# Recurrent scan in one kernel: key norms kept as twelve columns of tokens, and cumulative differences taken in the middle of the previous block's inversion

## What is computed

```
kk = hs(k0 * k_k)                                   # heads of 64 channels
kk = kk / jnp.maximum(jnp.sqrt(jnp.sum(kk * kk, axis=-1, keepdims=True)), 1e-12)
k  = hs(k0 * (1.0 + (a - 1.0) * k_a))
bonus = jnp.sum(rh * k * r_k, axis=-1, keepdims=True) * vh
# per token, for each direction d:
sa = jnp.einsum('bhij,bhj->bhi', s, kk_t)
s = s * w_t[:, :, None, :] - sa[..., None] * b_t[:, :, None, :] + v_t[..., None] * k_t[:, :, None, :]
y = jnp.einsum('bhij,bhj->bhi', s, r_t)
```

## Time and profile before

| what | value |
|---|---|
| median of 3 runs | 3482.51 us (3479.51 to 3484.06) |
| profiled execution, its own time | 3481.5 us |
| its span | 3479.7 us |
| PE busy | 3148.1 us, 90% |
| DVE busy | 1621.9 us, 47% |
| POOL busy | 1338.8 us, 38% |
| ACT busy | 1193.3 us, 34% |
| scan stage in the span | 2310 to 2930 us |

### The profile page before, as it was taken

How to read it: one execution, slowest core, us unless ns; L and a number is a source line. 1 busy time by engine, 2 the same in 40 slices (tenths; PEclk the granted TensorE clock), 3 DMA queues, 4 the chain that set the end, 5 groups by cost and what they waited for, 6 DMA issues and landing times. The chain is left out here.

```text
span 3479.7 us, 51376 instructions
## 1 busy us (share of the span) xinstructions
PE 3148.1 (90%) x19551; PEld 2515.4 (72%) x19551; DVE 1621.9 (47%) x3054; ACT 1193.3 (34%) x2127; POOL 1338.8 (38%) x880
## 2 busy tenths in 40 slices
PE   6999989799998999899899979995788889979996
PEld 5888865588886888677688858873666666758875
DVE  6444377444435673422621134326666645264443
ACT  3222245422223222234322232243444434343342
POOL 3444431344443434433344432234666630133332
PEclk8999989899998999999899989996999989979998
DMA  7565421365544554222433341222222233111211
GB/s 230 176 190 162 131 70 43 97 187 181 170 144 140 173 159 150 87 86 73 127 92 96 95 140 49 66 87 60 49 52 52 52 102 109 37 54 56 61 49 43
DMA packets 636834, 363.16 MB, mean 104 GB/s; under 512 B 109182, under 2 KB 629108, under 8 KB 636144
## 3 DMA queue, kind: packets, MB, share of 16 engines
q1 hardware_dynamic: 632432, 353.48, 34.3%
q10 hardware_dynamic: 3056, 6.29, 0.5%
q0 software_dynamic: 1168, 0.91, 0.1%
HBM read 334.12 MB, written 26.50 MB: 104 GB/s over the span
## 5 line engine op out<-in xcount | busy, mean ns | idle before, releaser
L266 POOL TENSOR_TENSOR w_lo<-w_raw,w_hi 128x1024 fp32r<-128x1024 f32 (+1 forms) x398 | 939.6, 2362 | 1724.9 <-ACT w_hi L258 1724.9
L303 PE MATMUL acc<-h,w_hi 128*128 128x512 f32 x3136 | 979.2, 393 | 6.7 <-POOL w_lo L266 6.7
L258 ACT ACTIVATE w_hi<-w_raw 128x1024 fp32r<-128x1024 f32 (+1 forms) x398 | 414.5, 1042 | 989.4 <-PE acc L303 961.3
L303 PEld LDWEIGHTS acc<-h,w_hi 128*128 128x128 f32 x3136 | 584.1, 188 | 128.7 <-POOL w_lo L266 7.8
L303 PE MATMUL acc<-h,w_lo 128*128 128x512 f32 x1568 | 613.3, 391 | 0.0
L303 PE MATMUL acc<-hid,w_hi 128*128 128x512 f32 x1408 | 437.1, 392 | 0.0
L303 PE MATMUL lat<-h,w_hi 128*128 128x512 f32 x912 | 336.6, 408 | 19.6 <-DVE h L429 17.5
L303 PEld LDWEIGHTS acc<-h,w_lo 128*128 128x128 f32 x1568 | 294.9, 188 | 63.9
L830 DVE SCALAR_TENSOR_TENSOR ada_part<-ada_raw,c_act,ada_part 128x256 f32<-128x256 f32 x672 | 315.0, 488 | 18.6
L303 PEld LDWEIGHTS acc<-hid,w_hi 128*128 128x128 f32 x1408 | 263.5, 188 | 54.1
L303 PE MATMUL acc<-hid,w_lo 128*128 128x512 f32 x704 | 275.0, 391 | 0.0
(11 more groups left out here) (512 smaller groups left out, 4866.2 us busy)
## 6 DMA issues: line engine op xcount, KB each, us to landing
w_raw<-in_ffn_w SPq DMA_DIRECT2D x240, 512.0 KB, 4.0
ada_raw<-in_ada_w SPq DMA_DIRECT2D x88, 1024.0 KB, 5.0
w_raw<-in_od_w_in SPq DMA_DIRECT2D x32, 512.0 KB, 4.0
w_raw<-in_ev_w_in SPq DMA_DIRECT2D x30, 512.0 KB, 3.9
w_raw<-in_ffn_w SPq DMA_DIRECT2D x32, 384.0 KB, 3.5
image<-inverse_wait SPq DMA_DIRECT2D x288, 32.0 KB, 2.2
first_ada<-in_ada_w SPq DMA_DIRECT2D x8, 1024.0 KB, 12.4
w_raw<-in_ab_w_in SPq DMA_DIRECT2D x16, 512.0 KB, 3.8
```

What stands on the lines that cost most here:

```text
L258: act.activation(K.w_hi[:, first % SPLIT, 0:tiles, :], K.raw[:, first % RAW, 0:tiles, :], ACT.Copy).then_inc(K.hi_ready, 1)
L266: pool.tensor_tensor(K.w_lo[:, first % SPLIT, 0:tiles, :], K.raw[:, first % RAW, 0:tiles, :], K.w_hi[:, first % SPLIT, 0:tiles, :].bitcast ...
L303: mm = pe.matmul(out, w[:, slot, k, :], moving(ap, k, tokens), start=first and k == 0 and p == 0, stop=last and k == tiles - 1 and p == le ...
```

## The change

1. `norm` becomes twelve small products: 64 tokens of `tmp` as the stationary operand, two columns of `bd64` as the moving one, so that tokens lie on partitions and the sums of one block are 12 columns (`inv`, 128x12). ACT's root, DVE's maximum and one reciprocal work on these 12 columns. A new PE operation `spread` (twelve products of a broadcast column with the identity) brings the factors back to PSUM by tiles of 64x128, and DVE multiplies `kk` with them (`unit`) in place of POOL's `kk`. After the root ACT evaluates one sigmoid of a single column (`warm`), for c > 0.
2. POOL's two differences of block `c + 1` are taken in `invert(c)`, after round n = 21 (`2 * N // 3`); for blocks 0 and 1 just ahead of their preparation. POOL's list has nine operations left.
3. The places move: DVE's maximum, reciprocal and sums earlier, `kt` and `k` from n = 16 to 19 to n = 18 to 21, `rk` from 26 to 31, the bonus product on PE from 29 to 32 and the bonus on DVE from 32 to 34; the gates of `decay` on ACT one place earlier, those of `rate` one later (15 and 17). `lora(1, 0)` now waits for DVE's `unit`, and `spread` for `decay1` and `inv`. On ACT the second rate gate of block 0 thereby falls behind `late(1)`.

```diff
-    "pe": ["norm", "decay0", "decay1", "rate0", "rate1", "bonus"],
+    "pe": ["norm", "decay0", "decay1", "spread", "rate0", "rate1", "bonus"],
@@ gpsimd
+                def differences(c):
+                    O = B[c % 3]
+                    for d in range(2):
+                        pool.wait_ge(S.pd, prep("dve", c, f"sum{d}"))
+                        pool.tensor_tensor(O.q[d], O.cs[d], O.q[d], ALU.subtract).then_inc(S.pq, 1)
...
+                        if n == 2 * N // 3 and c + 1 < RB:
+                            differences(c + 1)
                     pool.wait_ge(S.solving, base + 2 * N - 2)
                     pool.sem_inc(S.solved, 1)
...
+                    op("ksum", tmp, O.kt[0], O.kt[1], ALU.add, ("dve", "k1"))
                     for d in range(2):
-                        op(f"before{d}", q[d], O.cs[d], q[d], ALU.subtract, ("dve", f"sum{d}"))
-                    op("kk", kk, kk, tmp, ALU.mult, ("dve", "inv"))
-                    op("ksum", tmp, O.kt[0], O.kt[1], ALU.add, ("dve", "k1"), ("pool", "kk"))
-                    for d in range(2):
-                        op(f"bkk{d}", rate[d], rate[d], kk, ALU.mult, ("dve", f"kt{d}"), ("pool", "kk"))
+                        op(f"bkk{d}", rate[d], rate[d], kk, ALU.mult, ("dve", f"kt{d}"))
...
+                split("before0")
+                differences(0)
                 prepare(0, split)
...
+                differences(1)
                 prepare(1)
@@ tensor
                     if n == 6:
-                        product(K.bd64, lambda sl: tmp[:, sl], act("square"), *([(S.low_copied, c * 2 * PAIRS)] if c else []))
-                    if n == 9:
+                        pe.wait_ge(*act("square"))
+                        if c:
+                            pe.wait_ge(S.low_copied, c * 2 * PAIRS)
+                        for ch in range(NCH):
+                            for m, a in enumerate(SIDES):
+                                half = slice(ch * CH + 64 * m, ch * CH + 64 * m + 64)
+                                mm = pe.matmul(prep_bank[a, 0, 2 * ch:2 * ch + 2], tmp[:, half], K.bd64[:, 0:P:64],
+                                               start=True, stop=True)
+                        mm.then_inc(S.pp, 1)
+                    if n == 8:
                         lora(0, 0, (S.lw, c * 64 + 64), act("root"))
-                    if n == 11:
+                    if n == 10:
                         lora(0, 1, act("decay0"))
-                    if n == 13:
-                        lora(1, 0, act("decay1"))
-                    if n == 15:
+                    if n == 12:
+                        pe.wait_ge(*act("decay1"))
+                        pe.wait_ge(S.pd, prep("dve", c, "inv"))
+                        for ch in range(NCH):
+                            for h, a in enumerate(SIDES):
+                                mm = pe.matmul(prep_bank[a, ch // 3, ch % 3 * CH:ch % 3 * CH + CH],
+                                               inv[:, 2 * ch + h:2 * ch + h + 1].broadcast_to([P, 64]), K.ident,
+                                               start=True, stop=True)
+                        mm.then_inc(S.pp, 1)
+                    if n == 14:
+                        lora(1, 0, (S.pd, prep("dve", c, "unit")))
+                    if n == 16:
                         lora(1, 1, act("rate0"))
-                    if n == 29:
+                    if n == 32:
                         product(K.bd64, lambda sl: tmp[:, sl], act("rate1"), (S.pd, prep("dve", c, "rk")),
...
-                places = {3: 6, 7: 9, 10: 11, 12: 13, 14: 15}
+                places = {3: 6, 7: 8, 9: 10, 11: 12, 13: 14, 15: 16}
@@ scalar
                     if n == 7:
-                        op(tmp, None, ACT.Sqrt, pe("norm"))
+                        op(inv[:], prep_bank[:, 0, 0:2 * NCH], ACT.Sqrt, pe("norm"))
+                        if c:
+                            act.activation(warm[:], K.ones[:, 0:1], ACT.Sigmoid)
                     for d in range(2):
-                        if n == 10 + 2 * d:
+                        if n == 9 + 2 * d:
                             gate(O.q, f"decay{d}", "w0", d)
-                        if n == 14 + 2 * d:
+                        if n == 15 + 2 * d:
                             gate(O.rate, f"rate{d}", "a0", d)
-                        if n == 17 + d:
+                        if n == 18 + d:
                             power(wi[d], O.cs[d], 1, dve(f"sum{d}"))
...
-                for n in range(11):
+                for n in range(10):
                     prepare(0, n)
                 late(0)
-                for n in range(11, 17):
+                for n in range(10, 17):
                     prepare(0, n)
                 late(1)
@@ vector
-                    if n == 9:
+                    if n == 8:
                         act("root")
-                        done(dve.tensor_scalar(tmp, tmp, 1e-12, None, ALU.max))
-                    if 9 <= n < 15:
+                        done(dve.tensor_scalar(inv[:], inv[:], 1e-12, None, ALU.max))
                         own("max")
-                        sl = slice((n - 9) * CH, (n - 8) * CH)
-                        inverse = dve.reciprocal(tmp[:, sl], tmp[:, sl])
-                    if 11 <= n < 15:
-                        sums((n - 11) % 2, (n - 11) // 2)
-                    if n == 14:
-                        done(inverse)
+                        done(dve.reciprocal(inv[:], inv[:]))
+                    if 10 <= n < 14:
+                        sums(n % 2, (n - 10) // 2)
+                    if n == 13:
+                        own("kk")
+                        dve.wait_ge(S.pp, prep("pe", c, "spread"))
+                        by = prep_bank[:, :, 0:THREE]
+                        done(dve.tensor_tensor(kk.rearrange("p (a t) -> p a t", a=2), kk.rearrange("p (a t) -> p a t", a=2), by,
+                                               ALU.mult))
                     for d in range(2):
-                        if n == 16 + d:
+                        if n == 18 + d:
                             act("rate1")
...
-                        if n == 18 + d:
+                        if n == 20 + d:
                             own(f"kt{d}")
...
-                    if n == 26:
+                    if n == 31:
                         dve.wait_ge(S.pq, prep("pool", c, "ksum"))
                         done(dve.scalar_tensor_tensor(tmp, tmp, col("r_k"), row(0), ALU.mult, ALU.mult))
-                    if n == 32:
+                    if n == 34:
                         own("r1")
                         dve.wait_ge(S.pp, prep("pe", c, "bonus"))
```

More of the change, by code:

```diff
@@ L2119, in even_scan_phase @@
         masks = S.sb("masks", [P, 4, P])
+        warm, inv = S.sb("warm", [P, 1]), K.inv_norm
         level = S.sb("level", [P, 2, 64])
@@ L2596, in _ @@
                     multiply(pe, K, seg, i, i, 0, DB, late_ps(n), lambda p, k, sl: K.h[:, p, k, sl], before=before)
-                prepare(0, 29)
+                prepare(0, 32)
                 blocks(prepare, lambda c, n: c and invert(c, n), begin, step)
@@ L3604, in second_block @@
             K.w_inv = K.sbuf(scan, "w_inv", [P, TOK])
-            K.lora_w = K.sbuf(scan, "lora_w", [P, 4, P])
+            K.lora_w = K.sbuf(scan, "lora_w", [P, 2, P])
+            K.inv_norm = K.sbuf(scan, "inv_norm", [P, 2 * TOK // CH])
             K.mixed = K.sbuf(scan, "mixed", [P, 2 * D])
```

## The result

The changed kernel takes 3496.0 us (median of 6 runs, 3493.6 to 3498.9) against 3482.1 us for the kernel before in the same comparison: ratio 1.004, 95% interval 1.0030 to 1.0051. It is slower by about 14 us. The forecast was 3482.0 us with a range up to 3493; the result lies above it.

The account below looks back on a forecast made before the run. The prediction took the ring to close each cycle: 80.1 + 3.6 + 2.0 = 85.7 us against 88.9, 12.8 less in four. With + 13 for the head the sum was 0: 3482.0 us, range 3465 to 3493.

Parts of the forecast that it names:

- the bonus product: PE's product moved into the cycle's last stretch: + 2.0 us a cycle, between 1.5 and 2.9 by PE's clock.
- the lock: POOL's operations on SBUF hold up one of DVE's; the forecast sum had no term for this during the inversion.
- the ring: Chain from low copies through gather, inversion, transpose, scatter, images, cross product to next block: 80.1 us bare, 85.7 after.
- the tail: Blocks 4 and 5, which have no preparation: forecast to stay as they were, 0 us.
- The head: Preparation of blocks 0 and 1 up to the first low copy: + 13 us (8.5 to 18), from 6 and 7.
- the inversion: POOL's substitution in each cycle: left at 39.7 us, with 3.6 us added for the two differences.
- The stall: ACT's four waits at n = 23 for POOL's first difference, 23.4 us in all: forecast to go.
- The slower rival: Half clock in every cycle and a full head of 16 us: + 9, about 3491 us, chance 0.22.

Follow-up runs that it names:

- a_bonus: The changed kernel with `rk`, the bonus product and the bonus at their old places (26, 29, 32): 3474.3 us, ratio 0.9978 to the kernel before.
- a_pieces: The changed kernel with POOL's two differences cut into twelve pieces, one behind each of rounds 12 to 23: 3489.8 us, ratio 1.0018 to the kernel before.
- e_rk: c_pieces with `rk` at 28 instead of 26 and the bonus product at 30 instead of 29: 3466.2 us, ratio 0.9967 to the kernel before.
- c_split: a_bonus with POOL's two differences whole but apart, behind rounds 17 and 23 instead of both behind 21: 3474.5 us, ratio 0.9974.
- f_dve: e_rk with block 0's second rate gate and transpose moved earlier on ACT, and both differences on DVE instead of POOL: 3449.5 us, ratio 0.9902.
- c_pieces: a_bonus with POOL's two differences cut into twelve pieces of 128 columns, behind rounds 12 to 23: 3473.4 us, ratio 0.9976.

## Why the prediction was wrong

Three things were wrong: the lock, which the sum had at nothing, two stretches of the ring, which were mis-sized, and the tail, which also stood at nothing.

- **The head** was right in sum and in its two pieces. `ksum` of block 0 starts at 2345.24, 5.2 us later by the square (forecast 6), behind the second gate:

```profile
2339.77 1.28 ACT L2650 ACT_TABLE_LOAD   x1
2341.07 1.05 ACT L2650 ACTIVATE q_r_rate<-prep,params 128x384 f32<-128x384 f32 x2
...
2345.24 1.86 POOL L2334 TENSOR_TENSOR x_context<-x 128x768 f32<-128x768 f32 x1 [3.01 <-DVE x L2829]
```

  Block 1 adds 6.7 (forecast 7), and a_bonus takes 6.6 off, so most of it is `rk` and the bonus product at the end of DVE's chain. In detail it was less exact: behind the inversion the first images come 8.8 us later (forecast 8), but `br` comes 2.1 us later (18.5 us against 16.4), outside the forecast of 1.5 early to 0.7 late. The product itself takes 2.90 us at 2441.31, the 2.9 of the earlier trace rows. The extra table load is followed by its gate at once; no drain shows, as before.
- **The stall** at n = 23 went, as forecast. **The step that failed** is "`kt` and `k` weigh down step 3 instead. All of this comes before the wait at n = 27 and is hidden by it: by my estimate ACT comes there 2 to 3 us ahead of the inversion's end". I priced POOL's two operations by what they cost POOL (3.6 us) and not by what they do to DVE. They held a DVE operation for 3.3 to 3.9 us in each cycle, PE ran dry, and ACT came 2.0 to 5.6 us late. By a_pieces that is 7.3 us in four cycles of the 14.1 that I was off. The sign was in my own rows: in the head I read that the `k` pair took 4.03 us beside POOL's operations, and used it there alone.
- **The bonus product** was mis-sized. The ring's three stretches show it, as means of the four cycles:

  | stretch of a cycle | forecast | a_pieces | changed | e_rk |
  |---|---|---|---|---|
  | low copy to POOL's first operation | 17.2 | 18.0 | 17.6 | 17.7 |
  | inversion, with the differences | 43.3 | 43.2 | 42.8 | 43.0 |
  | inversion's end to the next low copy | 25.2 | 26.2 | 28.8 | 23.7 |
  | sum | 85.7 | 87.4 | 89.2 | 84.4 |

  In a_pieces nothing but the ring closes the cycle: ACT waits for the inversion in all four. Its last stretch is 3.0 us longer than the 23.2 without a product, where I took 2.0, within the ends that I gave (1.5 and 3.5). I had `rk` run while the images land; in the changed kernel PE waits for it in three of four cycles (0.97, 1.75 and 1.14 us), and the product takes 2.25 us on average. In e_rk, with both two or three places earlier, the stretch is 0.5 above the bare one. So the 14.1 us in four cycles are 7.3 for the lock, 3.9 for the product and `rk`, 3.3 for a first stretch that I took from the third cycle alone, and 0.3 less in the inversion. That these add up is so by construction; only the first is a comparison of two kernels. The ring itself was rightly found, and a_pieces' 87.4 stands just above my upper end of 87.2.
- **The tail**: "Blocks 4 and 5 have no preparation and stay" was wrong. I moved the bonus past two slots and did not ask who waits for it; SyncE does, once. The tail measured + 3.5 us where I had 0, and a_late, in which SyncE's wait stands behind the sends, has 3.4 less; the kernels with the bonus at 32 have 1 to 5 less.
- **The slower rival** had the half clock and a full head; of its signs the clock was right (0.90). Its mark "if the images came 2 us later still" with 3496 hits the time by luck: ACT's transpose came late for another reason, the head was 11.9 and not 16, and by the rival's own terms (a head of 16, nothing gained) it would be 3482 + 16 = 3498.
- **The inversion** was rightly left alone. a_tiny has the six reciprocals gone and POOL's differences on one column, and its inversion takes 39.6 to 39.8 us against 39.4 to 39.7. So nothing came off, as the prediction had it.

On SBUF the prediction held that no row tests who shuts out whom. Now rows do, in the third and, most plainly, the first cycle, where the DVE operation (`kt0`) is the one that takes 0.75 us in a_pieces:

```profile
2494.22 4.60 DVE L2826 TENSOR_SCALAR mixed<-q_r_rate,params,one_minus_ka 128x768 f32<-128x768 f32 x1
```

```profile
2494.84 3.57 POOL L2305 TENSOR_TENSOR q_r_rate<-q_r_rate 128x768 f32<-128x768 f32 x2
```

POOL's two subtractions take 3.57 us in both, their time alone (3.56 in the kernel before), and DVE's operation waits for both of them. The conversion from `rate` to `kt`, one SBUF tensor in, waits as the product with two does (3.92 against 0.67 in c_split). The one `br` that a difference met, with one input in PSUM, didn't wait (c_split). The Trainium skill's page "SBUF — State Buffer" (section "SBUF: two separate sides") calls this an exclusive lock, held for a whole instruction against DVE operations with two SBUF inputs or in a two-port mode. The rows agree with the lock; whether `kt` runs in such a mode they don't show. They disagree on the length, if it is read as one instruction: the loser waited for two in a row, 3.57 us.

## What to carry to other kernels

An operation moved into an engine's idle time is priced three times: on its own engine, on the engine that it holds up at that moment (here DVE, by 3.5 us), and on every queue that waits for its signal, SyncE's included. Where a loop has several near-equal limits, each removed stall uncovers the next (here lock, `ksum`, transpose, each within 4 us); read after each cut what ACT, DVE and PE wait for, since the gain of a single cut says nothing of the pair. The differences were cheapest on DVE itself: 0.9 us each in the head and 1.2 in the cycles (f_dve), against 1.8 on POOL and 3.5 of DVE's time lost to the pair.

## What the runs showed of the hardware

- A DVE operation recorded as started 0.09 us ahead of POOL's pair (2675.13 against 2675.22) still ended only 0.82 us after it, and one recorded 0.62 us ahead (2494.22 against 2494.84), nearly its whole time alone, ended 0.41 after it: the order of the records doesn't say who is held up.
- The same subtractions, moved to other rounds (c_split) or cut into pieces of 128 columns (c_pieces), cost DVE's keys operations little: they average 0.96 and 1.06 us there, at most 1.34 (c_pieces), against 0.95 alone.
